# Copying the attention scores to SBUF in VectorE's pass for the minima

## The reference

```python
def diff_attend(q, k, v, lam):                       # layer 0: 8 heads with two maps each
    s = jnp.einsum('bqhmd,bkhmd->bhmqk', q, k).astype(jnp.float32) * ATTN_SCALE
    p = jax.nn.softmax(s, axis=-1)
    w = (p[:, :, 0] - lam * p[:, :, 1]).astype(v.dtype)
    return jnp.einsum('bhqk,bkhe->bqhe', w, v)
...
        # layer 1: 16 heads, a neighbourhood in the grid with a bias, and the context
        s_loc = jnp.where(col_in[None, None, :, None, :], s_loc + bias[None].astype(jnp.float32), -jnp.inf)
        s_ctx = jnp.einsum('bqhd,bkhd->bhqk', q_row, k_c).astype(jnp.float32) * ATTN_SCALE
        s_all = jnp.concatenate([s_loc.reshape(B, NA_HEADS, GRID_W, n_loc), s_ctx], axis=-1)
        prob = jax.nn.softmax(s_all, axis=-1).astype(v_band.dtype)
```

## Time and profile before

| what | value |
|---|---|
| median of 3 runs | 3874.09 us (3874.08 to 3877.96) |
| span of the profiled execution | 3870.4 us, mean granted TensorE clock 0.985 |
| its own time | not given apart; the runs' lowest time, 3874.08 us, less the span leaves 3.7 us around it |
| busy in the span: PE, PEld | 3668.5 us (95%), 2984.9 us (77%) |
| DVE, ACT, POOL | 2209.8 us (57%), 1338.7 us (35%), 833.0 us (22%) |
| first attention stage | 256 to 464 us |
| second | 1302 to 1473 us |
| third | 2036 to 2234 us |

### The profile page before, as it was taken

How to read it: one execution, slowest core, us unless ns; L and a number is a source line. 1 busy time by engine, 2 the same in 40 slices (tenths; PEclk the granted TensorE clock), 3 DMA queues, 4 the chain that set the end, 5 groups by cost and what they waited for, 6 DMA issues and landing times. The chain is left out here.

```text
span 3870.4 us, 54090 instructions
## 1 busy us (share of the span) xinstructions
PE 3668.5 (95%) x20171; PEld 2984.9 (77%) x20171; DVE 2209.8 (57%) x3167; ACT 1338.7 (35%) x2342; POOL 833.0 (22%) x588
## 2 busy tenths in 40 slices
PE   7988899999999899999999999999989998899998
PEld 5876688888878677777786678888878876687886
DVE  5746646556573475444436647656665637846445
ACT  3346532121243454222325522212123334523222
POOL 2500012313132111222220011221310007901222
PEclk9999999999999999999999999999999999999999
DMA  5134223322322311544320013233221141032222
GB/s 183 66 120 131 66 77 115 114 100 102 113 67 68 85 45 42 188 152 155 113 65 10 1 44 135 104 113 114 105 74 55 57 142 33 23 109 96 98 93 72
DMA packets 191993, 352.38 MB, mean 91 GB/s; under 512 B 42236, under 2 KB 43853, under 8 KB 191821
## 3 DMA queue, kind: packets, MB, share of 16 engines
q1 hardware_dynamic: 187693, 340.83, 26.4%
q10 hardware_dynamic: 4144, 9.44, 0.7%
HBM read 341.71 MB, written 16.92 MB: 93 GB/s over the span
## 5 line engine op out<-in xcount | busy, mean ns | idle before, releaser
L569 POOL TENSOR_TENSOR x<-x,scaled_buf 128x512 f32<-128x512 f32 (+1 forms) x360 | 495.1, 1391 | 2202.1 <-DVE scaled_buf L561 2201.7
L129 DVE TENSOR_TENSOR w_lo<-raw,w_hi 128x2048 fp32r<-128x2048 f32 x198 | 465.6, 2351 | 685.0 <-ACT w_hi L123 675.7
L123 ACT ACTIVATE w_hi<-raw 128x2048 fp32r<-128x2048 f32 x197 | 377.1, 1914 | 1286.3 <-PE psum L386 1283.9
L384 PE MATMUL psum<-hT_hi,w_hi 128*128 128x512 f32 (+1 forms) x1888 | 669.0, 354 | 2.4 <-DVE hT_lo L848 1.5
L385 PE MATMUL psum<-hT_lo,w_hi 128*128 128x512 f32 (+1 forms) x1888 | 665.1, 352 | 0.0
L386 PE MATMUL psum<-hT_hi,w_lo 128*128 128x512 f32 (+1 forms) x1888 | 664.5, 352 | 0.0
L384 PE MATMUL psum<-w_hi,uT_hi 128*128 128x512 f32 x1280 | 503.0, 393 | 0.0
L386 PE MATMUL psum<-w_hi,uT_lo 128*128 128x512 f32 x1280 | 498.7, 390 | 0.0
L385 PE MATMUL psum<-w_lo,uT_hi 128*128 128x512 f32 x1280 | 498.2, 389 | 0.0
L561 DVE TENSOR_TENSOR scaled_buf<-psum,gate 128x512 f32<-128x512 f32 x360 | 244.8, 688 | 337.3 <-PE psum L386 291.9
L384 PE MATMUL psum<-w_hi,hT_hi 128*128 128x512 f32 x1072 | 419.8, 392 | 2.2 <-issue 1.2
(11 more groups left out here) (286 smaller groups left out, 4918.4 us busy)
## 6 DMA issues: line engine op xcount, KB each, us to landing
raw<-in_w_mlp SPq DMA_DIRECT2D x64, 1024.0 KB, 5.2
raw<-in_ff_w SPq DMA_DIRECT2D x64, 1024.0 KB, 5.3
mod_wide<-in_w_mod SPq DMA_DIRECT2D x32, 1536.0 KB, 8.5
mod_wide<-in_w_mod SPq DMA_DIRECT2D x8, 3072.0 KB, 10.5
raw<-in_ssm_w_in SPq DMA_DIRECT2D x20, 1024.0 KB, 5.1
mod_slab<-in_w_mod SPq DMA_DIRECT2D x8, 2048.0 KB, 8.4
raw<-in_a_w_qkv SPq DMA_DIRECT2D x12, 1024.0 KB, 5.1
raw<-in_b_w_qkv SPq DMA_DIRECT2D x12, 1024.0 KB, 5.1
```

Of the source, the lines that this page charges most:

```text
L123: act.activation(K.w_hi[h][:, :, :], K.raw[h][:, :, :], ACT.Copy).then_inc(K.hi_done.h, 1)
L129: dve.tensor_tensor(K.w_lo[h][:, :, :], K.raw[h][:, :, :], K.w_hi[h][:, :, :].bitcast(F32), ALU.subtract).then_inc(K.lo_done.h, 1)
L384: pe.matmul(out, hi_a, hi_w, start=first, stop=False, **check)
L569: pool.tensor_tensor(x, x, K.scaled_buf[:, j % 2, :], ALU.add).then_inc(K.added.h, 1)
```

## The change

The pass over the scores that takes the minima now also writes them to `p_mat` in SBUF, and the Exp reads and writes `p_mat` in place.

- The one or two reductions become two `tensor_scalar` instructions (`taken`): times 1.0, minimum with 3e38, an accumulated minimum, output to `p_mat`. With the bias, the two custom instructions write to `p_mat` instead of PSUM, and the context columns are passed in two instructions of 256 columns.
- A new semaphore `s_read` counts the units whose PSUM set has been read. `scores_early(v)` waits for `s_read(v - 2)` in place of `p_done`. In the first stage the Exp waits for it too, in place of `nm_done`.
- The wait for the buffer of `p_mat` (the transposes of unit v - 3) moves from ScalarE to VectorE, in front of the pass.

```diff
@@ def scores_early(v)
-                pe.wait_ge(K.p_done.h, at(K.p_done, 2 * (v - 2) + 1))
+                pe.wait_ge(K.s_read.h, at(K.s_read, v - 2))
@@ def probabilities(v)
-                act.wait_ge(K.nm_done.h, at(K.nm_done, v))
-
-                if v >= 3:
-                    for b in range(2):
-                        if last_turn(v - 3, b) is not None:
-                            act.wait_ge(K.pt_done[b].h, at(K.pt_done[b], last_turn(v - 3, b)))
+                low = K.nm_done if bias or sink else K.s_read
+                act.wait_ge(low.h, at(low, v))
                 if sink:
                     act.activation(K.sink_exp[:, v % 4, :], K.sink_exp[:, v % 4, :], ACT.Exp)
                 for m in range(2):
-                    act.activation(K.p_mat[:, v % 3, u.span(m)], S(v)[:, u.span(m)], ACT.Exp, bias=K.neg_max[:, v % 4, m:m + 1],
+                    p = K.p_mat[:, v % 3, u.span(m)]
+                    act.activation(p, p, ACT.Exp, bias=K.neg_max[:, v % 4, m:m + 1],
                                    scale=-1.0, accum_out=K.p_sum[:, v % 4, m:m + 1]).then_inc(K.p_done.h, 1)
@@ def minima(v)
                 dve.wait_ge(K.s_done.h, at(K.s_done, v))
+                if v >= 3:
+                    for b in range(2):
+                        if last_turn(v - 3, b) is not None:
+                            dve.wait_ge(K.pt_done[b].h, at(K.pt_done[b], last_turn(v - 3, b)))
                 nm = K.neg_max[:, v % 4, :]
-                s = S(v)
+                s, p = S(v), K.p_mat[:, v % 3, :]
+                taken = lambda span, low: dve.tensor_scalar(p[:, span], s[:, span], 1.0, 3e38, ALU.mult, ALU.min, accum_out=low)
                 if bias:
...
                     for m in range(2):
-                        x = s[:, 0:4 * P] if m == 0 else s[:, 8 * P:12 * P]
+                        span = slice(8 * m * P, (8 * m + 4) * P)
                         g = K.G[u.pair % 2][:, m, row:row + N_ROWS, :].rearrange("p r c -> p (r c)")
-                        dve.tensor_tensor_reduce(x, x, g, 1.0, 3e38, ALU.add, ALU.min, nm[:, m:m + 1])
-                    link(dve.tensor_reduce(K.ctx_min[:, v % 4, :], s[:, 4 * P:8 * P].rearrange("p (m c) -> p m c", m=2), AX.X, ALU.min))
+                        dve.tensor_tensor_reduce(p[:, span], s[:, span], g, 1.0, 3e38, ALU.add, ALU.min, nm[:, m:m + 1])
+                    for m in range(2):
+                        ins = taken(slice((4 + 2 * m) * P, (6 + 2 * m) * P), K.ctx_min[:, v % 4, m:m + 1])
+                    ins.then_inc(K.s_read.h, 1)
+                    dve.wait_ge(K.s_read.h, at(K.s_read, v))
                     dve.tensor_tensor(nm, nm, K.ctx_min[:, v % 4, :], ALU.min).then_inc(K.nm_done.h, 1)
                     return
-                if u.nk == 6:
-                    ins = dve.tensor_reduce(nm, s.rearrange("p (m c) -> p m c", m=2), AX.X, ALU.min)
-                else:
-                    for m in range(2):
-                        ins = dve.tensor_reduce(nm[:, m:m + 1], s[:, u.span(m)], AX.X, ALU.min)
+                for m in range(2):
+                    ins = taken(u.span(m), nm[:, m:m + 1])
+                ins.then_inc(K.s_read.h, 1)
                 if sink:
-                    link(ins)
+                    dve.wait_ge(K.s_read.h, at(K.s_read, v))
...
-                ins.then_inc(K.nm_done.h, 1)
+                    ins.then_inc(K.nm_done.h, 1)
```

More of the change, by code:

```diff
@@ L1659, in attention_stage @@
     chunks = [u.chunks(heads) for u in units]
-    base = {s: s.n for s in (K.s_done, K.nm_done, K.p_done, K.inv_done, K.w_done, K.o_done, K.o_read, K.g_ready,
+    base = {s: s.n for s in (K.s_done, K.s_read, K.nm_done, K.p_done, K.inv_done, K.w_done, K.o_done, K.o_read, K.g_ready,
                              K.pt_done[0], K.pt_done[1], K.pt_read[0], K.pt_read[1], K.mod_used)}
@@ L1952, in _ @@
             K.dve_chain.n += link.k
-    for s in (K.s_done, K.nm_done, K.inv_done, K.o_done, K.o_read):
+    for s in (K.s_done, K.s_read, K.inv_done, K.o_done, K.o_read):
         s.n += N
+    if bias or sink:
+        K.nm_done.n += N
     K.p_done.n += 2 * N
@@ L3080, in program @@
         K.s_done = sem("s_done")
+        K.s_read = sem("s_read")
         K.nm_done = sem("nm_done")
```

## The result

The changed kernel takes 3883.99 us in the median of 7 runs (3875.43 to 3886.91), the kernel before 3874.09 us in its 7 (3872.48 to 3880.2). The ratio is 1.0021 with an interval of 1.0011 to 1.003: slower by some 8 us (the medians are 9.9 us apart), at the edge of what can be told from no change. The profiled execution is the fastest of the changed kernel's runs: span 3873.6 us and 3875.43 us in all, with a mean granted clock of 0.985, as before. Its span is only 3.2 us longer. The other six runs had a clock of 0.980 to 0.982 and spans of 3879.9 to 3885.1 us. So there are two things to explain: 3.2 us at the same clock, and the rest.

A forecast was written before the change was run, and what follows sets the result against it. TensorE, busy in 95% of the span, was taken as the bound, so VectorE and ScalarE act only through its waits. Stages one to three at +2.7, +0.3 and +2.5 us gave +5.5 on 3874.1: 3879.6 us, range 3867 to 3891.

The forecast's parts named there:

- The freed scores meet the next wait: Stage one: scores freed 0.55 and 0.32 us earlier only lengthen TensorE's waits on finish and the modulation's sum; no gain.
- Rival A: Stage one: the freed scores count and all 9.0 us of waiting for the Exp go; 3865.1 us, chance 0.12.
- The pass: VectorE's copying minima pass: about +0.12 us before the next instruction for a long unit, +0.07 us for a short one.
- Rival B: VectorE's accumulator reads stand alone: +0.20 us more per long unit's pass, +0.10 per sink; 3886.5 us, chance 0.27.
- The Exp: ScalarE's Exp reading SBUF instead of PSUM: +0.03 us each, +0.06 us for a unit.
- Stage one, +2.7 us: Stage one: 0.42 us more per pair, 3.3 us for 8, less about 0.6 us gained at the start.
- the 0.42 worked out: Loss per pair in stage one: 0.24 at the modulation's sum, 0.06 for the Exp, 0.12 at transposes behind finish.
- the 0.6 of the start: Start of stage one: scores that waited 0.69 us have nothing holding behind them, a real gain of about 0.6 us.
- Stage two, +0.3 us: Stage two: VectorE's 0.22 us more per unit fits in 0.34 us spare; only the start adds 0.22 + 0.06.
- Stage three, +2.5 us: Stage three: 16 waits on finish at 0.12 us make 1.9, plus 0.4 allowance and 0.2 at the start.
- The sum: Whole kernel: the three stages' losses together, +5.5 us on 3874.1 us, giving 3879.6 us.
- +0.24 us straight onto TensorE: Stage one: two long passes in the chain before the modulation's sum delay TensorE by 0.24 us, 8 times.

The follow-up runs named there:

- a2: Changed kernel with the scores waiting again for both Exps of the unit two before, not for VectorE's pass; 3883.81 us.
- e3: Kernel before plus an unused VectorE reduction of 256 columns ahead of the modulation's sum, 8 times in stage one; 3885.41 us.
- d1: Changed kernel with VectorE's modulation sum and add moved ahead of the minima pass in stage one; 3881.29 us.
- d3: Changed kernel with stage one's finish moved ahead of the reciprocal and the modulation's sum and add ahead of the minima pass; 3857.38 us.
- d4: Kernel before with stage one's finish moved ahead of the reciprocal and the modulation's sum and add ahead of the minima pass; 3859.95 us.
- a1: Changed kernel run again with no edit; 3881.49 us, ratio to the kernel before 1.0006 to 1.0024.
- c1: Changed kernel with VectorE's finish of stage one moved ahead of the reciprocal that waits for the Exp; 3892.47 us.

## Why the prediction was right, and where by luck

The forecast was a small loss, 3879.6 us in 3867 to 3891, and the sign, the size and the range were right. By its steps:

- **The freed scores meet the next wait.** Right. 0.55 us earlier at one place, and finish took 0.98 (0.84 plus the Exp, as worked out); the sum's wait is 1.72 us (1.25 + 0.32 + 0.24 = 1.81 worked out). The totals foreseen, about 13 and 5 us, are 12.4 and 5.4. Rival A fell with the profile and with a2 (25.45 us a pair without the release, 25.44 with it).
- **The pass.** +0.09 us for a long unit (1.76 against 1.67), taken as 0.12. The read of the accumulator is 0.08 us where the nearest rows had 0.14, and the instruction behind comes after 0.61 us at 512 columns in both cases. Rival B fell: the reads overlap. The prediction read the section on the DRAIN in the Trainium skill's "VectorE: DVE Perf Modes" as speaking for B. The section has the next instruction wait until the pipe is empty, but adds that one which isn't held starts earlier, and that second case is what the rows show.
- **The Exp.** +27 ns for 768 columns, taken as 30. The 43 ns worked out from the errata table of that page of the Trainium skill are too many here.
- **Stage one, +2.7 us.** The last transposes of the modulation begin at 455.1 us instead of 453.2, with the stage's start 0.2 us earlier: +2.1 us. A pair takes 25.44 us against 25.10, +0.34 for the 0.42 worked out, and the stage's first product of the modulation starts 0.7 us earlier in the stage, for the 0.6 of the start.
- **Stage two, +0.3 us.** From the first custom instruction to the last it is 163.7 us against 163.3. Right in its size, but VectorE's work grew less than worked out: from the first custom instruction to the last minimum it takes 2.03 us (before 1.98), not 0.22 more, and finish's last instruction starts 2.58 us behind it (before 2.59), so no spare time was needed.
- **Stage three, +2.5 us.** Mis-sized. The time from the first scores to the last transposes is 196.2 us in both profiles, with 3.4 us less at the low clock after, which at 0.3 to 0.4 us each hides 1.0 to 1.4 us. I had put +0.12 us on each chain. By the trace after it is 1.34 us against 1.32 for two passes of 512 columns, since both the read and the gap to the second pass are shorter than in the rows of stage two that I took.
- **The sum.** +5.5 us of schedule were forecast and +3.2 measured at the same mean clock. That the median nevertheless lies 4.4 us above my value is due to a term that I didn't have: the clock. I wrote that a gain or a loss arises only from TensorE's waits, and priced a longer wait at its own length. In this kernel a longer wait in stage one also brings time at the lower level of the clock, at 0.3 to 0.4 us for each; a pair of the changed kernel that it hits takes up to 1.7 us more, several times the 0.34 us of the longer pair itself. The step that failed is therefore "+0.24 us straight onto TensorE": it was too cheap. That the value came within 4.4 us was luck in part: a schedule taken too large by 2.3 us and a clock not taken at all have opposite signs.

What stays open: what exactly pulls the granted clock down. The runs show that longer pauses suffice (e3), that pauses of no more than 1.13 us can be followed by it as well (d1), that it goes from nearly all pairs when the long pauses go (d3, d4), and that one and the same program can fall on either side (the profile after and a1). Open too is how much of the 0.43 us a pair that the change gains in d3 is the release alone.

## What to carry to other kernels

Before you free a buffer earlier, look at what the consumer waits for right behind: here two waits on VectorE's order of work took back all of it, and moving two small steps in that order was worth 16 us in the kernel before (3859.95 against 3875.95, timed together) and some 24 us in the changed one (3857.4 against 3881.5, on two chips). Neither step alone did it in the changed kernel (c1, d1). A pause of a busy TensorE is to be priced above its own length when the granted clock is seen to fall behind such pauses, and it's the profile's clock by stretch, over several runs, that tells. To part the two, measure the period of a repeated piece of work where the granted clock is 1.00 throughout: here it is the same within 0.01 us from pair to pair, where whole runs of one kernel scatter by 10 us. In this kernel a pass that copies and reduces 1536 columns costs as much as the reduction, within 0.1 us.

## What the runs showed of the hardware

The clock is the surprise. One instruction more of 0.42 us on VectorE, eight times in 3874 us, makes the schedule 3.9 us longer and the median 11.7 us, three times as much (e3; by the interval 6.2 us at least). The same program runs at a mean granted clock of 0.985 or 0.981, 9.3 us apart, with no wait longer. And a custom instruction that adds, keeps a minimum and reads its accumulator is quicker with its output in SBUF than in PSUM: 689 ns and 84 for the read, against 716 and 142 in the kernel before, here first:

```profile
L1887 DVE CUSTOM_DVE_ANT_0 psum<-psum,G 128x512 f32<-128x512 f32 x64 | 43.1, 716 | 21.8 <-PE psum L1729 21.8
...
L1887 DVE DVE_READ_ACCUMULATOR2_ANT neg_max<- 128x1 f32 x64 | 9.1, 142 | 0.0
```

```profile
L1889 DVE CUSTOM_DVE_ANT_0 p_mat<-psum,G 128x512 f32<-128x512 f32 x64 | 41.7, 689 | 21.8 <-PE psum L1729 21.8
...
L1889 DVE DVE_READ_ACCUMULATOR2_ANT neg_max<- 128x1 f32 x64 | 5.3, 84 | 0.0
```
